# Moving the masked blocks and the scaling of q in the DeltaNet inverse from GpSimd to VectorE

## What is computed

```python
decay = jnp.exp(jnp.where(tri, gcum[..., :, None] - gcum[..., None, :], -jnp.inf))
kk = jnp.einsum('bhnid,bhnjd->bhnij', kc, kc)
a_strict = jnp.where(strict, bc[..., :, None] * kk * decay, 0.0)
lhs = a_strict + jnp.eye(c, dtype=f32)
sol = lax.linalg.triangular_solve(lhs, rhs, left_side=True, lower=True, unit_diagonal=True)
q_dec = qc * jnp.exp(gcum)[..., None]
```

## Time and profile before

| | us |
|---|---|
| median of 3 runs | 2168.74 |
| lowest and highest | 2163.32, 2169.66 |
| the profiled execution | 2169.72 |
| its span, first to last instruction | 2167.8 |

### The profile page before, as it was taken

One profiled execution on the slowest core, in us unless ns is written; L12 is line 12 of the kernel. 1 busy time (PEld: TensorE's weight loads), 2 busy tenths in 40 slices (PEclk: granted clock), 3 DMA queues, 4 the chain that ended last, 5 costly groups with the idle time before them and its releaser, 6 DMA issues.

```text
span 2167.8 us, 27272 instructions
## 1 busy us (share of the span) xinstructions
PE 2026.0 (93%) x10014; PEld 1611.8 (74%) x10014; DVE 903.5 (42%) x1202; ACT 736.1 (34%) x1125; POOL 101.6 (5%) x71
## 2 busy tenths in 40 slices
PE   7999999998999999998898999779999999999994
PEld 5886776677868778786586888558888888888883
DVE  5715456546244262541145562453223323323335
ACT  5325555444343343532233332333113103202310
POOL 0000000000203012030000000100000000000002
PEclk9999999999999999999899999889999999999997
DMA  4231221213031121212325433111111111111113
GB/s 162 101 107 69 87 76 70 87 67 127 20 121 44 39 107 39 77 39 104 135 97 195 136 122 142 59 58 48 50 47 48 48 48 48 48 48 49 48 39 155
DMA packets 52763, 174.18 MB, mean 80 GB/s; under 512 B 5744, under 2 KB 5744, under 8 KB 52720
## 3 DMA queue, kind: packets, MB, share of 16 engines
q1 hardware_dynamic: 51568, 171.52, 22.2%
q10 hardware_dynamic: 1152, 2.10, 0.3%
HBM read 127.45 MB, written 46.14 MB: 80 GB/s over the span
## 4 chain that ended last, share of the span: by engine, by line
PE 73%; DVE 6%; ACT 4%; issue 3%; DMA 3%; POOL 1%; SPq 1%; DVEq 0%; POOLq 0%; ACTq 0%
PE gemm L320 18%; PE gemm L322 18%; PE gemm L321 18%; PE dn L1187 2%; PE z L1083 2%; PE dn L1185 2%; PE gemm L1266 2%; DMA w_raw<-w_stream 2%; PE gemm L1267 2%; PE gemm L1268 2%; PE dn L1105 1%; DVE d_cv L1474 1%; ACT w_hi L307 1%; PE attn_out L1116 1%; PE cumsum L1116 1%
## 5 line engine op out<-in xcount | busy, mean ns | idle before, releaser
L320 PE MATMUL gemm<-act_hi,w_hi 128*128 128x512 f32 x1472 | 616.7, 419 | 18.4 <-DVE act_lo L501 10.2
L322 PE MATMUL gemm<-act_hi,w_lo 128*128 128x512 f32 x1472 | 580.4, 394 | 0.0
L321 PE MATMUL gemm<-act_lo,w_hi 128*128 128x512 f32 x1472 | 579.6, 394 | 0.0
L320 PEld LDWEIGHTS gemm<-act_hi,w_hi 128*128 128x128 f32 x1472 | 280.1, 190 | 94.5 <-issue 29.5
L312 DVE TENSOR_TENSOR w_lo<-w_raw,w_hi 128x1024 fp32r<-128x1024 f32 x142 | 175.1, 1233 | 398.0 <-ACT w_hi L307 393.1
L322 PEld LDWEIGHTS gemm<-act_hi,w_lo 128*128 128x128 f32 x1472 | 279.5, 190 | 61.1
L321 PEld LDWEIGHTS gemm<-act_lo,w_hi 128*128 128x128 f32 x1472 | 280.8, 191 | 54.2 <-issue 6.5
L307 ACT ACTIVATE w_hi<-w_raw 128x1024 fp32r<-128x1024 f32 x142 | 149.6, 1053 | 329.7 <-PE gemm L322 281.4
L320 PE MATMUL gemm<-f_hi,w_hi 128*128 128x512 f32 x512 | 199.2, 389 | 0.0
L321 PE MATMUL gemm<-f_lo,w_hi 128*128 128x512 f32 x512 | 199.2, 389 | 0.0
L322 PE MATMUL gemm<-f_hi,w_lo 128*128 128x512 f32 x512 | 199.2, 389 | 0.0
(11 more groups left out here) (231 smaller groups left out, 2374.7 us busy)
## 6 DMA issues: line engine op xcount, KB each, us to landing
w_raw<-w_stream SPq DMA_DIRECT2D x142, 512.0 KB, 3.6
projections<-stage SPq DMA_DIRECT2D x60, 512.0 KB, 2.9
gate<-projections SPq DMA_DIRECT2D x48, 256.0 KB, 2.7
d_in<-projections SPq DMA_DIRECT2D x12, 512.0 KB, 4.5
y_lo<-branch_outputs SPq DMA_DIRECT2D x6, 1024.0 KB, 11.9
x_sb<-xT SPq DMA_DIRECT2D x8, 512.0 KB, 9.6
x_fin<-xT SPq DMA_DIRECT2D x4, 1024.0 KB, 9.3
residual<-mixed SPq DMA_DIRECT2D x8, 512.0 KB, 2.6
```

Of the source, the lines that this page charges most:

```text
L320: nc.tensor.matmul(g_bank[hf][:], w_hi[s][:, k, :], a_hi[:, k, t], start=(k == 0), stop=False)
L321: nc.tensor.matmul(g_bank[hf][:], w_hi[s][:, k, :], a_lo[:, k, t], start=False, stop=False)
L322: last = nc.tensor.matmul(g_bank[hf][:], w_lo[s][:, k, :], a_hi[:, k, t], start=False, stop=(k == KT - 1))
```

## The change

VectorE gets a helper that writes d_B for a level and a group. It is called with level 1 at the end of the code of stage vT of each group, followed by the scaling of that group's half of q, and in each stage x of levels 1 to 5 it writes the mask of the next level, after a wait for that x product. GpSimd's loop over the heads is gone. The waits of PE for dn_b and dn_q stay as they are.

```diff
+                def level_mask(lev, g):
+                    c = slice(4 * g, 4 * g + 4)
+                    nc.vector.tensor_tensor(d_B[:, c, :], d_at[:, c, :], mask(consts[:, C_LEV + lev, :]), ALU.mult).then_inc(dn_b[g], 1)
+
                 local = [0]
                 for x, name in enumerate(DN_STAGES):
                     for g in range(2):
...
                             nc.vector.tensor_tensor(d_TT[:, c, :], d_TT[:, c, :], p3, ALU.subtract).then_inc(dn_taken[g], 1)
+                        if name == "vT":
+                            level_mask(1, g)
+                            q3 = d_cv[0][:, HALF * g:HALF * g + HALF].rearrange("p (n c) -> p n c", c=P)
+                            nc.vector.tensor_tensor(q3, q3, d_eg[:, c, :], ALU.mult).then_inc(dn_q, 1)
+                        if name[0] == "x" and name != f"x{N_LEV - 1}":
+                            dve.wait_ge(dn_prod[g], DN_USES * i + 3 + x)
+                            level_mask(int(name[1:]) + 1, g)
                         beside()
...
-            with pool.Fori(0, 4) as i:
-                for lev in range(1, N_LEV):
-                    for g in range(2):
-                        c = slice(4 * g, 4 * g + 4)
-                        if lev == 1:
-                            pool.wait_ge(dn_taken[g], 1 + DN_USES * i + 3 + DN_STAGES.index("gram"))
-                        else:
-                            pool.wait_ge(dn_prod[g], DN_USES * i + 3 + DN_STAGES.index(f"x{lev - 1}"))
-                        nc.gpsimd.tensor_tensor(d_B[:, c, :], d_at[:, c, :], consts[:, None, C_LEV + lev, :].broadcast_to([P, 4, P]),
-                                                ALU.mult).then_inc(dn_b[g], 1)
-                    if lev == 1:
-                        for g in range(2):
-                            c = slice(4 * g, 4 * g + 4)
-                            q3 = d_cv[0][:, HALF * g:HALF * g + HALF].rearrange("p (n c) -> p n c", c=P)
-                            pool.wait_ge(dn_prod[g], DN_USES * i + 3 + DN_STAGES.index("qk"))
-                            nc.gpsimd.tensor_tensor(q3, q3, d_eg[:, c, :], ALU.mult).then_inc(dn_q, 1)
```

## The result

| us | before | after |
|---|---|---|
| median | 2169.14 (6 runs) | 2176.64 (6 runs) |
| lowest to highest | 2163.32 to 2173.36 | 2174.33 to 2178.98 |
| profiled execution | 2169.72 | 2178.98 |
| its span | 2167.8 | 2177.2 |

The ratio is 1.0037, with a 95% interval of 1.0021 to 1.0053: 7.5 us slower between the medians, 8.0 by the ratio, where 7.4 had been worked out and 2177.1 forecast.

The account below looks back on a forecast made before the run. TensorE, busy 93% of the span, nearly bounds the kernel, and GpSimd's work is hidden. Stalls of 4.8 us at stage vT and 2.6 at level 2 add 7.4 to 2169.72, giving 2177.1 us, range 2172 to 2180.5.

Parts of the forecast that it names:

- The sum: Over four heads: 4.8 us at stage vT plus 2.6 at level 2, together 7.4 us slower.
- What an instruction costs on VectorE: Each added mask or scaling on VectorE delays the next instruction by 0.60 us, with 0.72 as the upper end.
- D: Rival: each added VectorE instruction holds the next for 0.72 us and w_lo stays at 1.52; 2180.2 us, chance 0.11.
- Place 1: Stage vT: group 0's mask and q scaling delay group 1's L1527 and TensorE's t0; 1.20 us a head, at most 1.44.
- Place 2: Stages x of levels 1, 3, 4, 5: masks fit VectorE's idle time before the subtractions; cost nothing up to 0.9 us.
- Place 3: Level 2: both level 3 masks stand between w_lo and group 0's subtraction, delaying TensorE's t2; 0.64 us a head.
- B: Rival: only one of the two stalls, at stage vT, is paid; 2174.5 us, chance 0.14.
- C: Rival: delays absorbed, as the head's end hangs on something outside VectorE's list, like a weight load; 2169.7 us, chance 0.12.
- E: Rival: faster, as TensorE's 2.2 us of "issue" before x1 really wait for GpSimd; 2166.3 us, chance 0.08.
- The range: The forecast's bounds for the changed kernel's time: 2172 to 2180.5 us.

Follow-up runs that it names:

- vt_only: Kernel before with only level 1's masks and the scaling of q moved to VectorE, levels 2 to 6 staying on GpSimd; ratio 1.0017 to the kernel before.
- late3: Changed kernel with level 3's masks written after each subtraction of stage y2 instead of in stage x2; ratio 1.0022 to the kernel before.
- late3_t0: late3 with level 1's masks and the scaling of q moved behind group 1's L1529, in stage t0; ratio 1.0004 to the kernel before.
- twice: Changed kernel with one more 128x512 product into scratch ahead of each mask of levels 2, 4, 5 and 6; ratio 1.0030 to the kernel before.
- x_only: Kernel before with only the masks of levels 2 to 6 moved to VectorE, level 1 and q staying on GpSimd; ratio 1.0013 to the kernel before.
- early_pool: Kernel before with only the two instructions making level 0 of d_TT moved from stage vT to qk, GpSimd keeping its work; ratio 1.0026 to the kernel before.
- early_late3: late3 with the two instructions making level 0 of d_TT moved from stage vT into stage qk; ratio 0.9993 to the kernel before.
- early_qlate: early_pool, but GpSimd scales q after its masks of level 4 instead of level 1; ratio 1.0000 to the kernel before.

## Why the prediction was right

**The sum.** 7.4 us was worked out, 7.5 measured between the medians, and 7.4 found in the trace as the sum of eight steps. That the medians meet the sum to 0.1 is luck, as the interval goes from 4.6 to 11.5 us; the steps are the evidence. Heads as wholes did not lengthen by 1.84 alone, as the forecast's 132.9 for 131.0 had it: from t0 to t0 of the next head the three distances grew by 2.21, 3.06 and 1.91, because the waits outside the stages lie between. In the kernel before these distances are 131.67, 130.86 and 129.60; what repeats to a few hundredths is the stages inside a head, and not the heads.

**What an instruction costs on VectorE.** 0.60 was taken from the distance of two starts and not the 0.69 of a record, and the eight steps bear it out: 1.20 to 1.22 for two at stage vT. The forecast's D, the 0.72 of a chained pair and an unchanged w_lo, would have given steps of 1.44 and 1.18 and 10.5 us.

**Place 1**, 1.20 a head: right, alone in vt_only and late3, absent in late3_t0.

**Place 2**, nothing: right, but its cushion was read too small. The forecast had it that a mask over 0.9 us would push each subtraction and so the time. The run twice pushes the subtractions of group 0 by 0.3 and more and costs nothing, because TensorE waits next for group 1's, or has a filler step to do. It takes about three masks in the place of one before the time moves. The step that fell short is the one from "the subtraction is late" to "the time is longer"; it carried no part of the sum.

**Place 3**, 0.64 a head: right, alone in x_only, absent in late3. In it stood the assumption that w_lo comes back from 1.52 to 1.23 when GpSimd is idle; x_only and vt_only show both values, and in the changed kernel none of the 22 lasts over 1.23.

**The forecast's rivals.** Its B, one of the two paid, and C, absorbed, are out: eight steps of full size. E, that GpSimd's slowness was waited for, is out too: the 2.2 us of "issue" ahead of level 1's x products stand unchanged in the changed kernel's list of waits (PEld dn L1185, 2.2 us in four), where GpSimd has nothing left to do in the heads. That GpSimd is about twice as slow per instruction, 1.3 against 0.69, was true and worth nothing, as nobody waited for it.

**The range** was wider than the mechanism needed and about right for the measurement: single executions of the changed kernel run from 2174.33 to 2178.98.

## What to carry to other kernels

Before work goes to an engine that "only waits", look at what stands behind each place in its list and ask whether that is what another engine waits for next; a share of 43% says nothing on it. In this kernel the price of an unchained instruction was the distance of starts, 0.60 us, and its free room went up to the next thing that TensorE really waits for. The same 56 instructions cost 7.5 us in one order and nothing that can be told from none in another, and what removed the stalls was a place behind the instruction that is waited for.

## What the runs showed that had not been expected

VectorE and GpSimd slow each other when both read two operands from SBUF: beside GpSimd's products VectorE's 128x512 product goes from 0.68 to between 0.99 and 1.28 us, its L1524 from 0.69 to up to 1.67, its 128x1024 subtraction from 1.23 to 1.53, and GpSimd's two scalings of q from some 2.6 to 3.45 us. The subtractions L1531, which take one operand from PSUM, kept 0.69 (686 to 690 ns in all 48) although some ran beside a mask of GpSimd, as that of 817.76 does. The Trainium skill ("SBUF — State Buffer", "Who interferes with whom") has it that a Vector instruction with two inputs in SBUF contends with a GpSimd instruction that reads SBUF, and that one with at most one input there, outside the engine's two-port modes, does not. The traces agree with both halves, by the figures just given. The forecast used the rule for one instruction; what was new is its size as an effect on the whole, when VectorE's work is moved in time. Two instructions moved to an earlier place lose 5.6 us when they meet GpSimd's scalings of q (early_pool), and nothing when GpSimd is idle (early_late3) or scales q later (early_qlate). So GpSimd's work was free in the kernel before only as long as VectorE's list kept its order, and whoever tunes that list afterwards has to look at what GpSimd does at the same time, or have it do nothing.
